# The second layer's embedding product is computed at the end of the first layer and kept in SBUF

## The reference

```python
for i in range(DEPTH):                        # DEPTH = 2
    xn = rms_norm(h, norm_pre[i])
    if i < N_A:                               # layer 0
        y = rwkv7_time_mix(xn, ...)
    else:                                     # layer 1
        k_sh, v_sh = shared_kv(h, kv_norm, kv_w, cos, sin)
        y = diff_attention_mix(xn, k_sh, v_sh, b_w_in[j], ..., b_w_out[j], lam_init, cos, sin)
    h = h + rms_norm(y, norm_post[i])
    e = p[i] @ ple_w[i]                       # p[i]: 256 x 256, ple_w[i]: 256 x 1024
    g = jax.nn.sigmoid(h @ ple_gate[i])       # ple_gate[i]: 1024 x 1024
    h = h + rms_norm(g * e, ple_norm[i])
```

## Time and profile before

| | us |
|---|---|
| median of 3 runs | 1073.95 |
| lowest, highest | 1072.15, 1075.27 |
| profiled execution | 1075.32 |
| its span | 1073.5 |
| PE busy, of the span | 1034.9 (96%) |
| POOL busy | 744.8 (69%) |
| ACT busy | 557.8 (52%) |
| DVE busy | 479.2 (45%) |

### The profile page before, as it was taken

One profiled execution on the slowest core, in us unless ns is written; L12 is line 12 of the kernel. 1 busy time (PEld: TensorE's weight loads), 2 busy tenths in 40 slices (PEclk: granted clock), 3 DMA queues, 4 the chain that ended last, 5 costly groups with the idle time before them and its releaser, 6 DMA issues.

```text
span 1073.5 us, 20351 instructions
## 1 busy us (share of the span) xinstructions
PE 1034.9 (96%) x8566; PEld 868.0 (81%) x8566; DVE 479.2 (45%) x674; ACT 557.8 (52%) x890; POOL 744.8 (69%) x470
## 2 busy tenths in 40 slices
PE   7999999999999999999999999999999999999896
PEld 6888899999979969999998456699986787887675
DVE  3125275331136967411115958544467344223433
ACT  6557365444446957444453344222344468578835
POOL 5986559998866689988882165440327787998853
PEclk9999999999999999999999999999999999999999
DMA  9762445555555654555556335300004463644241
GB/s 357 276 235 79 147 160 179 184 195 179 194 170 166 212 171 159 185 194 184 189 185 245 100 127 178 127 4 4 4 22 142 149 234 120 212 162 136 98 131 76
DMA packets 46218, 168.36 MB, mean 157 GB/s; under 512 B 5648, under 2 KB 5904, under 8 KB 45872
## 3 DMA queue, kind: packets, MB, share of 16 engines
q1 hardware_dynamic: 43616, 158.02, 43.7%
q0 software_dynamic: 2512, 9.05, 2.5%
HBM read 166.00 MB, written 1.05 MB: 156 GB/s over the span
## 4 chain that ended last, share of the span: by engine, by line
PE 83%; ACT 7%; DVE 5%; POOL 2%; issue 2%; DMA 1%; SPq 0%; DVEq 0%; ACTq 0%
PE psum L482 26%; PE psum L519 19%; PE psum L743 16%; PE psum L494 5%; PE psum L2310 5%; POOL ring_r L833 2%; ACT high_r L1003 1%; PE psum L2462 1%; PE psum L288 1%; DMA h<-x 1%; PE psum L2028 1%; PE psum L2376 1%; PE psum L2198 1%; ACT arena L1050 0%; PE psum L2088 0%
## 5 line engine op out<-in xcount | busy, mean ns | idle before, releaser
L833 POOL TENSOR_TENSOR ring_r<-ring,high_r 128x512 fp32r<-128x512 f32 (+1 forms) x374 | 644.7, 1757 | 152.5 <-ACT high_r L1003 140.0
L1003 ACT CAST high_r<-ring 128x1024 fp32r<-128x1024 f32 x250 | 258.0, 1048 | 183.0 <-DMA ring<-w 180.2
L519 PE MATMUL psum<-x_high,high_r 128*128 128x256 f32 x640 | 182.4, 285 | 2.8 <-DVE x_low L352 2.8
L519 PE MATMUL psum<-x_low,high_r 128*128 128x256 f32 x640 | 181.1, 283 | 0.0
L519 PE MATMUL psum<-x_high,ring_r 128*128 128x256 f32 x640 | 181.1, 283 | 0.0
L715 DVE TENSOR_TENSOR arena<-arena 128x512 f32<-128x512 f32 x32 | 43.7, 1366 | 201.0 <-ACT arena L691 200.9
L519 PEld LDWEIGHTS psum<-x_high,high_r 128*128 128x128 f32 x640 | 122.7, 192 | 4.1 <-issue 2.5
L519 PEld LDWEIGHTS psum<-x_low,high_r 128*128 128x128 f32 x640 | 122.7, 192 | 0.6
L519 PEld LDWEIGHTS psum<-x_high,ring_r 128*128 128x128 f32 x640 | 122.7, 192 | 0.0
L743 PE MATMUL psum<-high_r,zz_high 128*128 128x512 f32 x256 | 99.8, 390 | 1.3 <-DVE zz_low L722 1.3
L743 PE MATMUL psum<-ring_r,zz_high 128*128 128x512 f32 x256 | 99.8, 390 | 0.0
(11 more groups left out here) (363 smaller groups left out, 1881.6 us busy)
## 6 DMA issues: line engine op xcount, KB each, us to landing
ring<-w SPq DMA_DIRECT2D x288, 512.0 KB, 3.3
row<-rows POOLq DMA_DIRECT2D x14, 512.0 KB, 6.2
arena<-relt SPq DMA_DIRECT2D x2, 1536.0 KB, 13.3
h<-x SPq DMA_DIRECT2D x1, 1024.0 KB, 11.3
arena<-lora POOLq DMA_DIRECT2D x2, 512.0 KB, 5.4
out<-h SPq DMA_DIRECT2D x2, 512.0 KB, 2.7
arena<-xT SPq DMA_DIRECT2D x1, 768.0 KB, 6.8
con<-consts SPq DMA_DIRECT2D x1, 529.0 KB, 5.9
```

The source lines that it names most:

```text
L519: ins = nc.tensor.matmul(out, a, b, start=(k == 0 and q == 0), stop=(k == KT - 1 and q == 2))
L833: ins = nc.gpsimd.tensor_tensor(low(m)[:, part], raw(m)[:, part], read(high(m))[:, part], ALU.subtract)
L1003: nc.scalar.copy(high(m), raw(m)).then_inc(high_made, 1)
```

## The change

The second layer's embedding product moves to the border of the layers. Its ring tile W_PLE1 now follows the first layer's gate tiles, ahead of the fused product's 32 pieces, so these and all behind them up to the second out product stand four places later in the ring; the count of pieces is the same. The tile is laid out by column half: pieces 0 and 1 carry nothing, 2 and 3 hold the two halves. Its input pT comes right behind the first one's. TensorE runs the product in four parts of two f32 matmuls, in the places of the dummy matmuls, around the transposes. ScalarE copies the two column halves from PSUM to a tile of their own, e1, which lies where r_high did (r_high is done by then), and VectorE multiplies by e1 in the second layer's tail. TensorE's fused product waits for those copies, since it reuses the banks. The calls of `split_until` around the tails move.

```diff
--- before.py
+++ after.py
...
-W_RKVG, W_OUT_A, W_PLE0, W_KVQG, W_OUT_B, W_PLE1, W_TILES = 47, 55, 57, 60, 68, 70, 73
+W_RKVG, W_OUT_A, W_PLE0, W_GATES0, W_PLE1, W_KVQG, W_OUT_B, W_GATES1, W_TILES = 47, 55, 57, 58, 60, 61, 69, 71, 73
...
-UNUSED_PIECES = {4 * n + i for n in (W_PLE0, W_PLE1) for i in (2, 3)}
+UNUSED_PIECES = {4 * W_PLE0 + 2, 4 * W_PLE0 + 3, 4 * W_PLE1, 4 * W_PLE1 + 1}
...
-        r_high = ctx.enter_context(nc.sbuf_tensor("r_high", [P, KT, SEQ], F32R))
+        e1 = sb("e1", [P, NT, D])
+        r_high = nc.alloc_sbuf_tensor_at("r_high", [P, KT, SEQ], F32R, offset=nc.sbuf_base - 4 * NT * D, align_bytes=32)[:, :, :]
...
+        e1_taken = sem("e1_taken")
...
-        pT_sb = view(7 * S, 2, SEQ)
+        pT_sb, pT1_sb = view(7 * S, 2, SEQ), view(3 * S, 2, SEQ)
...
+            pool.dma_start(pT1_sb, pT[:, 1]).then_inc(lor_landed, 16)
...
-            low_until(4 * W_PLE1)
-            pool.wait_ge(od_ready, 2)
-            pool.dma_start(pT_sb, pT[:, 1]).then_inc(lor_landed, 16)
...
+                g0 = 4 * (W_GATES0, W_GATES1)[e_n]
+                if e_n == 1:
+                    split_until(g0 + 3)
...
-                    split_until(4 * first + 13 + t)
-
-            def embed(i, tile, e_n, T):
+                    split_until(g0 + 1 + t + 3 * e_n)
+
+            def embed(i, gates, e_n, T):
                 token_high(act, T, (0, 1))
-                split_until(4 * tile + 9)
+                split_until(4 * gates + 5)
...
-                split_until(4 * tile + 12)
-                used(act, tile + 1)
+                split_until(4 * gates + 8)
+                used(act, gates)
...
-                split_until(4 * tile + 15)
...
-                        used(act, tile + 2)
+                        used(act, gates + 1)
                     nc.scalar.activation(ge[:, t, HALF:D], psum[:, 6 + t, :], ACT.Sigmoid).then_inc(gate_act, 1)
+                    if e_n == 0 and t == 1:
+                        split_until(4 * W_KVQG + 1)
...
-            embed(7, W_PLE0, 0, T_H6)
-            split_until(4 * W_KVQG + 5)
+            embed(7, W_GATES0, 0, T_H6)
+
+            def take_e1(c):
+
+                used_piece(act, 4 * W_PLE1 + 2 + c)
+                nc.scalar.copy(e1[:, :, c * HALF:(c + 1) * HALF], pair_out(c)).then_inc(e1_taken, 1)
+
+            take_e1(0)
+            split_until(4 * W_KVQG + 2)
...
-            split_until(4 * W_KVQG + 8)
+            split_until(4 * W_KVQG + 4)
...
+            split_until(4 * W_KVQG + 5)
+            take_e1(1)
+            split_until(4 * W_KVQG + 6)
...
-            embed(10, W_PLE1, 1, T_H8)
+            embed(10, W_GATES1, 1, T_H8)
...
-                nc.vector.tensor_tensor(ge[:, :, 0:HALF], psum[:, 0:2, :], ge[:, :, 0:HALF], ALU.mult).then_inc(ge_ready, 1)
+                if e_n == 1:
+                    dve.wait_ge(e1_taken, 2)
+                nc.vector.tensor_tensor(ge[:, :, 0:HALF], psum[:, 0:2, :] if e_n == 0 else e1[:, :, 0:HALF], ge[:, :, 0:HALF],
+                                        ALU.mult).then_inc(ge_ready, 1)
...
-                    nc.vector.tensor_tensor(ge[:, t, HALF:D], psum[:, 2 + t, :], ge[:, t, HALF:D], ALU.mult).then_inc(ge_ready, 1)
+                    nc.vector.tensor_tensor(ge[:, t, HALF:D], psum[:, 2 + t, :] if e_n == 0 else e1[:, t, HALF:D], ge[:, t, HALF:D],
+                                            ALU.mult).then_inc(ge_ready, 1)
...
-            def embed_pe(tile, e_n, T):
-                pe.wait_ge(lor_landed, 48 + 16 * e_n)
+            def embed_pe(gates, e_n, T):
                 posted_rows = lambda b: pe.wait_ge(h_post, 4 * e_n + b + 1)
-                for i in range(4):
-                    piece_ready(pe, 4 * tile + i)
-                embedding_half(tile, e_n, 0)
+                if e_n == 0:
+                    pe.wait_ge(lor_landed, 64)
+                    for i in range(4):
+                        piece_ready(pe, 4 * W_PLE0 + i)
+                    embedding_half(W_PLE0, 0, 0)
                 pe_token_transposes(pe, T, h, 0, posted_rows)
-                embedding_half(tile, e_n, 1).then_inc(piece_used, 4)
+                if e_n == 0:
+                    embedding_half(W_PLE0, 0, 1).then_inc(piece_used, 4)
...
-                        piece_ready(pe, 4 * (tile + 1) + i)
+                        piece_ready(pe, 4 * gates + i)
                         bank_out(pe, 4 * T + 2 * t + i // 2)
-                        ins = pe_piece_of_tile(pe, tile + 1, i, 4, xT2, t)
+                        ins = pe_piece_of_tile(pe, gates, i, 4, xT2, t)
...
-                        piece_ready(pe, 4 * (tile + 2) + i)
-                        ins = pe_piece_of_tile(pe, tile + 2, i, 6, xT2, t)
+                        piece_ready(pe, 4 * (gates + 1) + i)
+                        ins = pe_piece_of_tile(pe, gates + 1, i, 6, xT2, t)
...
-            embed_pe(W_PLE0, 0, T_H6)
+            embed_pe(W_GATES0, 0, T_H6)
...
-            hold_clock(0, 8)
+
+            def second_embedding(c, t):
+
+                piece_ready(pe, 4 * W_PLE1 + 2 + c)
+                for k in range(2):
+                    ins = nc.tensor.matmul(psum[:, 2 * c + t, :], pT1_sb[:, k, t * P:(t + 1) * P],
+                                           raw(4 * W_PLE1 + 2 + c)[:, k * HALF:(k + 1) * HALF], start=(k == 0), stop=(k == 1))
+                return ins
+
+            for i in range(2):
+                piece_ready(pe, 4 * W_PLE1 + i)
+            second_embedding(0, 0)
+            second_embedding(0, 1).then_inc(piece_used, 3)
             pe_transposes_of_tile(pe, T_H7, h, 0, token_ready(0))
-            hold_clock(0, 14)
+            pe.wait_ge(ge_ready, 3)
+            second_embedding(1, 0)
             pe_transposes_of_tile(pe, T_H7, h, 1, token_ready(1))
+            second_embedding(1, 1).then_inc(piece_used, 1)
...
+                    if i == 0:
+                        pe.wait_ge(e1_taken, c + 1)
...
-            embed_pe(W_PLE1, 1, T_H8)
+            embed_pe(W_GATES1, 1, T_H8)
...
-        half = f("ple_w_2")[i].reshape(2, P, D).transpose(1, 0, 2).reshape(P, 2048)
-        tiles.append(np.concatenate([half, half], 1))
+        if i == 0:
+            half = f("ple_w_2")[0].reshape(2, P, D).transpose(1, 0, 2).reshape(P, 2048)
+            tiles.append(np.concatenate([half, half], 1))
...
+        if i == 0:
+            half = f("ple_w_2")[1].reshape(2, P, 2, HALF).transpose(1, 2, 0, 3).reshape(P, 2048)
+            tiles.append(np.concatenate([half, half], 1))
```

## The result

| | before | after |
|---|---|---|
| median of 17 runs, us | 1073.66 | 1076.41 |
| lowest, highest | 1072.15, 1075.86 | 1073.97, 1078.85 |
| profiled execution | 1075.32 | 1078.85 |
| its span | 1073.5 | 1077.0 |

The ratio is 1.0022, its interval [1.0013, 1.0030]: the changed kernel is about 2.4 us slower. That is the sign of the forecast and inside its range, and under the 0.3% that was called no change, but twice the 1.15 us of its sum. So the question is which terms are off. The profiled execution of the changed kernel is the slowest of its 17, so its trace shows a larger loss than the median does.

The account below looks back on a forecast made before the run. The prediction took TensorE, 83% of the chain that ended last, to bound the kernel. Border +2.75 and end -1.6 sum to +1.15 us on the median of 1073.95: 1075.1 us, range 1070.5 to 1078.4.

Parts of the forecast that it names:

- Two small edits cost nothing: First layer's out tile and GpSimd's queue: the second pT's extra DMA issue and GpSimd's moved waits and issue cost 0.
- The border: Between the layers: late weight pieces make TensorE start fused piece 12 later, +2.75 us; bounds -2.65 and +4.45.
- The two waits for ring_r: At the border: TensorE waits for GpSimd's low halves, 3.1 us before fused piece 8, about 1.8 before piece 12.
- the block of moments: ScalarE at the border: its squares end 1.0 us later, VectorE is last, and fused piece 6 is split behind it at 903.6.
- The clock fall at K0: Fused product's start: its first four pieces took 12.63 us for 10.88 before, 1.75 lost; full clock expected after the change.
- From K12 on, 0: Attention stage from fused piece 12: GpSimd makes a piece in 2.50 us against 2.72 of use, so the shift stays.
- The end, -1.6: Last stage: 3.3 us of the removed 6.83 is won, and a clock fall behind the hole takes 1.7 back.
- twice as long: Last stage: the bound with a clock fall of double length, leaving a gain of 0.
- rival 3: Last stage: no clock fall, so 2.75 - 3.3 = -0.55 us, 1073.4; chance 0.15.
- Products with e: VectorE, last stage: reading two SBUF tensors takes 1.28 us with GpSimd at work, 0.69 without; hidden, costing nothing.
- rival 1: Border: the pieces are in time, giving -2.65 there and 1069.7 to 1068.0 in all; chance 0.15.
- rival 2: TensorE's waits before fused pieces 8 and 12: a second, uncovered clock fall, +2.85 to +4.55, 1076.8 to 1078.5; chance 0.18.

Follow-up runs that it names:

- e2: Kernel before, plus the second pT's DMA issued right behind the first one's and used by nothing; ratio to before 1.0005 [0.9996, 1.0014].
- e3: Kernel before without the second layer's embedding product, so its output lacks that term; ratio to before 0.9985 [0.9974, 0.9996].
- e8: Changed kernel with small dummy matmuls in the last stage's hole, a repeat because the first run's trace was unusable; ratio to before 1.0000 [0.9987, 1.0013].
- e4: Changed kernel with pieces 6 and 7 of the fused product split ahead of the moments; ratio to before 1.0003 [0.9991, 1.0014].
- e1: Changed kernel with the second pT's DMA issued only after the first layer's tail; ratio to before 1.0005 [0.9995, 1.0015].
- e6: Changed kernel with the edits of e1 and e4 together; ratio to before 0.9996 [0.9986, 1.0005].
- e7: Changed kernel with the edits of e1, e4 and e8 together; median 1072.18 us, ratio to before 0.9987 [0.9977, 0.9997].

## Why the prediction was right in sign and short in size

- **"Two small edits cost nothing": failed.** The prediction priced the second pT as an issue on GpSimd, and the issue takes 0.54 us and delays nothing. Its 256 KB were not followed. They land among the ring's pieces just when ScalarE waits for one of them, with the square that TensorE needs behind it in its queue. Measured +1.40; +1.27 when added alone, gone when moved. This is the greater part of what was missing.
- **The border: right in mechanism, +2.15 measured for +2.75.** The two waits for ring_r, their places and the order of K6, the moments and the rotation came as written. But K12 started 46.88 behind G, where 47.6 was forecast (before: 44.87). The mis-sized term is the block of moments: K6's split was put at 21.9 behind G and started at 21.03. The prediction took VectorE's part in that block to end about when it had ended before; it ended 0.65 earlier, and ScalarE waited 0.24 for it in place of 1.50.
- **The clock fall at K0 was priced wrongly, and it did no harm.** The forecast took the fall in the trace of before as a loss of 1.75 that the change would win back. e2 and e3 show that it costs 0.6 and is not always there, because TensorE waits for ScalarE ahead of K12 without it. GpSimd's line sets K12 after the change, so the sum did not depend on it. That the border is 2.7 to 2.8 longer than in e2 and e3, which looks like the forecast's 2.75, is luck: K12 came 0.7 too early, and the kernel before was 0.6 faster there.
- **From K12 on, 0: right,** +0.03.
- **The end, -1.6: the mechanism was right and a term was mis-sized.** The removed product won 3.47 at full clock (forecast 3.3). The clock fall was put at 1.7 from two places in the trace before. In the changed kernel it was twelve steps of 0.427 in place of 0.227, 2.4, and 0.4 at its two edges: 40.67 - 37.88 (e8) = 2.8. In e4 it was 39.50 - 37.88 = 1.6. The bound "twice as long" covered both. Nor is it there each time: e1 and e6 ran the end as rival 3 has it. The Trainium skill, "TensorE: Matmul & The Clock Gate", section "HAM oscillation — how this bites in real kernels", has work behind a hole start cold; the runs agree in three executions of five.
- **Products with e: right.** 2.22 against 1.22 us, hidden. The Trainium skill, "SBUF — State Buffer", section "Who interferes with whom", on the port pair that GpSimd and a VectorE operation with two SBUF inputs hold in turn, agrees with these rows.
- **Rivals.** The pieces were not in time (rival 1). Half-rate stretches behind K8 came in e1, e4, e7 and e8 (clock 0.72 to 0.75 from 914 to 920) and not in the changed kernel or e6. They ended ahead of K12 and were covered, as rival 2 had it for that place; none stood behind K12 in any trace.

In the trace the forecast's errors are +1.40 in the tail, -0.60 in the border and +0.93 at the end: errors of both signs, which partly cancel. The timed difference, 2.4 [1.4, 3.2], is a mean over executions with and without the falls of the clock, so it need not equal the 2.89 of one of them. That it falls inside the forecast's range owes something to the range's width, which was made for clock falls and not for the DMA that was missed.

What stays open: what decides in a given execution whether the clock falls behind the hole. The changed kernel and e4, which fell, and e1 and e6, which did not, have the same instructions around it.

## What to carry to other kernels

When a step is moved, its transfers move too: give each DMA a price by what is in flight where it now lands and who waits there, not by its issue. Taking work from the busy engine wins only up to the next late input (3.47 of 6.83 here), and the hole it leaves can cost clock behind it (1.6 to 2.8 us); try small dummy matmuls in the hole. Compare by distances between starts that both traces have: the drift of an execution (up to 1.95 us at O1 here) and its clock falls are as large as the terms in dispute.

## What the runs showed of the hardware that was not expected

- Whether the clock falls behind a wait differs from one execution to the next. At the border, behind the same wait of 1.29, it was 0.57 from 891.3 to 895.3 in before and 1.00 in e2 and e3. Behind K8, after a wait of 2.77 or 2.78, it was 1.00 in the changed kernel and 0.72 in e1 and e8 (914 to 920).
- One more 256 KB transfer from GpSimd's queue, added alone (e2), made ScalarE's wait for a 512 KB piece on SyncE's queue 1.8 us longer (3.08 to 4.85), and the row load's landing went from 4.6 to 6.1.
- Behind the hole at the end of the changed kernel the clock was 0.50 for about 5 us, although TensorE was by then full of matmuls without a gap.
